# Activation parts and every work buffer behind them start 128 bytes higher in on-chip memory; no instruction is added, removed or reordered

## The reference, cut to what matters

```
h      = modulate(rms_norm(x)), modulate(rms_norm(ctx))      # modulation: silu(c) @ mod_w
x     += gate * rms_norm(gated_linear_attention(h))          # 4 heads, both directions, ctx state first
x     += gate * rms_norm(silu(h @ W_gate) * (h @ W_up) @ W_out)      # hidden width 2816
---- second block
proj   = (x * (1 + scale) + shift) @ w_in                    # 9232 columns
o_a    = gated_deltanet(conv(qkv_a), ...)                    # 8 heads, triangular solve per chunk
o_b    = chunk_band_attention(q_b, k_b, v_b, rel_bias)       # 16 heads
x      = layernorm(alpha * x + gate * ((g_a * o_a @ Wa + g_b * o_b @ Wb) @ w_o))
x      = layernorm(alpha * x + gate * ((silu(u_gate) * u_val) @ w_down)),  u = conv(h @ w_up)
```

## Time and profile before

| | us |
|---|---|
| median of 3 runs | 1036.68 (1034.71 to 1036.95) |
| the profiled execution, its own time | 1037.48 |
| its span, first to last instruction | 1035.7 |
| granted TensorE clock, mean over the span | 0.972 of full |

### The profile page before, as it was taken

The page is one execution under the profiler, slowest core; times in us unless marked ns, Lnnn a source line. Parts: engine busy times, 40 slices in busy tenths (PEclk is TensorE's granted clock), DMA queues, the critical chain, the costliest instruction groups (busy, mean ns, idle before and its releaser), DMA issues.

```text
span 1035.7 us, 19911 instructions
## 1 busy us (share of the span) xinstructions
PE 955.3 (92%) x8438; PEld 903.5 (87%) x8438; DVE 702.7 (68%) x1112; ACT 547.3 (53%) x829; POOL 27.0 (3%) x71
## 2 busy tenths in 40 slices
PE   4699999969999999799899999989998699999995
PEld 1489999869999999699699998978998499999994
DVE  2659937677777665888774543566568778888744
ACT  2658232654544435756736334466764466766434
POOL 2100000000000000400100000000000000000000
PEclk9899999989999999899999999999999799999997
DMA  9834656548888887257424336543457545656921
GB/s 333 283 102 148 246 197 211 196 131 272 278 271 277 286 274 265 82 182 250 130 91 145 124 129 147 184 144 122 140 188 248 177 130 178 196 185 199 326 91 41
DMA packets 57400, 196.78 MB, mean 190 GB/s; under 512 B 6096, under 2 KB 10592, under 8 KB 57056
## 3 DMA queue, kind: packets, MB, share of 16 engines
q1 hardware_dynamic: 51840, 187.72, 54.2%
q10 hardware_dynamic: 5216, 7.53, 2.8%
q0 software_dynamic: 256, 0.26, 0.1%
HBM read 194.43 MB, written 1.06 MB: 189 GB/s over the span
## 4 chain that ended last, share of the span: by engine, by line
PE 76%; DVE 13%; ACT 5%; DMA 2%; issue 2%; ACTq 0%; SPq 0%; DVEq 0%
PE panel_banks L399 65%; DVE w_lo L1460 3%; DVE mix_work L1802 3%; DMA raw<-in_panels 2%; PE work_banks L768 2%; ACT w_hi L946 2%; DVE raw L1493 1%; PE work_banks L596 1%; PE work_banks L697 1%; PE work_banks L739 1%; PE work_banks L556 1%; PE work_banks L529 1%; PE work_banks L851 1%; PE work_banks L796 1%; ACT gla_work L984 0%
## 5 line engine op out<-in xcount | busy, mean ns | idle before, releaser
L399 PE MATMUL panel_banks<-act_hi,w_hi 128*128 128x256 f32 (+1 forms) x1600 | 462.0, 289 | 25.9 <-DVE w_lo L1460 10.1
L399 PE MATMUL panel_banks<-act_lo,w_hi 128*128 128x256 f32 (+1 forms) x1600 | 454.0, 284 | 0.0
L399 PE MATMUL panel_banks<-act_hi,w_lo 128*128 128x256 f32 (+1 forms) x1600 | 453.5, 283 | 0.0
L1460 DVE TENSOR_TENSOR w_lo<-raw,w_hi 128x1024 fp32r<-128x1024 f32 x260 | 315.5, 1222 | 141.6 <-ACT w_hi L946 140.9
L946 ACT ACTIVATE w_hi<-raw 128x1024 fp32r<-128x1024 f32 x260 | 272.3, 1055 | 164.0 <-PE panel_banks L399 121.7
L399 PEld LDWEIGHTS panel_banks<-act_hi,w_hi 128*128 128x128 f32 x1600 | 303.8, 190 | 38.5 <-issue 20.7
L399 PEld LDWEIGHTS panel_banks<-act_lo,w_hi 128*128 128x128 f32 x1600 | 304.4, 190 | 1.9 <-issue 0.5
L399 PEld LDWEIGHTS panel_banks<-act_hi,w_lo 128*128 128x128 f32 x1600 | 303.9, 190 | 1.6
L399 PE MATMUL panel_banks<-hidden_hi,w_hi 128*128 128x256 f32 x352 | 98.6, 280 | 2.4 <-ACT hidden_hi L1165 2.4
L399 PE MATMUL panel_banks<-hidden_hi,w_lo 128*128 128x256 f32 x352 | 98.4, 279 | 0.0
L399 PE MATMUL panel_banks<-hidden_lo,w_hi 128*128 128x256 f32 x352 | 98.2, 279 | 0.0
(11 more groups left out here) (268 smaller groups left out, 974.7 us busy)
## 6 DMA issues: line engine op xcount, KB each, us to landing
raw<-in_panels SPq DMA_DIRECT2D x356, 512.0 KB, 5.1
mix_work<-delta_rows ACTq DMA_DIRECT2D x2, 1024.0 KB, 11.9
x_t<-in_x ACTq DMA_DIRECT2D x1, 1024.0 KB, 9.4
gla_work<-in_ctx_x ACTq DMA_DIRECT2D x1, 1024.0 KB, 14.5
mix_work<-in_rel_bias ACTq DMA_DIRECT2D x1, 1024.0 KB, 10.2
out_x<-ffn_work SPq DMA_DIRECT2D x4, 256.0 KB, 2.5
mix_work<-in_rel_bias ACTq DMA_DIRECT2D x1, 768.0 KB, 14.9
c_wide<-in_c_rows ACTq DMA_DIRECT2D x1, 512.0 KB, 4.0
```

The lines of the kernel that those rows point to most:

```text
L399: ins = pe.matmul(out_, a, b, start=start and p == 0, stop=stop and p == 2, skip_group_check=True)
L1460: dve.tensor_tensor(wlo[:, v_ % PARTS, :], raw[:, u % RAW, :], whi[:, v_ % PARTS, :].bitcast(F32), ALU.subtract)\
```

## The change

The unused tensor in front of the activation parts grows from 16 to 48 numbers:

```
-        sb("act_home", [P, 16])
+        sb("act_home", [P, 48])
```

## The result

| | before | changed |
|---|---|---|
| median, us | 1036.72 (1034.61 to 1038.37, 6 runs) | 1028.57 (1022.76 to 1031.02, 6 runs) |
| ratio | | 0.9911, 95% interval 0.9891 to 0.9931 |
| the profiled execution, its span | 1037.48, 1035.7 | 1027.39, 1025.6 |
| granted TensorE clock, mean | 0.972 | 0.966 |

The forecast was 1036.7 us, "no change that can be measured". The kernel became 0.9% faster. The time lies in the range, but the kernel did change, and clearly beyond the interval, where no change was forecast.

The account below looks back on a forecast made before the run. The kernel was taken to be bound by the number of matmuls times the distance between their starts. Terms (a), (b) and (c) were each 0, so 1037.5 us profiled, 1036.7 us as median, range 1024 to 1041.5 us.

Parts of the forecast that it names:

- term (a): Distance between three-pass matmul starts, one operand moved, weights not: change taken as 0, bounds +4.3 to -23.6 us.
- Nothing about the addresses changed there: In qkv near 490 us the rate slowed after one matmul some 15 ns late; so rate is a state.
- Two relations, 320 and 192, thus give the same pair of rates: Moved minus unmoved address modulo 512, in normal and swapped panels: both show fast and slow rates, supporting 0.
- Each instruction sweeps over all remainders wherever it starts: Moving tiles of 1,024 bytes and weight blocks of 512 cover all remainders modulo 512, supporting 0 for layout.
- (b): Duration of DVE and ACT instructions on moved buffers: taken as 0, bounds ±0.2 to ±2.2 us.
- (c): DMA transfers into moved buffers: taken as 0; DMA's whole share of the chain would be 21 us.
- Fast stretches are lost: Rival: restarts after other PE work leave the matmuls in the slow rhythm, +4.3 us, 1041.0 us; chance 0.12.
- One or two long stretches turn fast: Rival: long slow stretches such as ffn_in's 1,050 matmuls take the fast rhythm, 1028 to 1032 us; chance 0.10.
- The rhythm is a matter of layout after all: Rival: the new address relation is fast nearly everywhere, 1013 to 1024 us, about 1018; chance 0.11.
- A third, slower distance: Rival: weight and activation read streams disturb each other more, up to +27.9 us, 1064 us; chance 0.07.

Follow-up runs that it names:

- p256: Kernel before with the activation parts and all behind them 256 bytes higher; 1036.32 us, ratio 0.9993.
- p0: Kernel before without the unused tensor, activation parts and all behind them 64 bytes lower, operand distance 0 modulo 256; 1048.79 us, ratio 1.013.
- d112_act: Kernel before with act and hidden parts starting 48 bytes inside larger tensors, weights left at 128 modulo 256, distance 112; 1025.04 us, on repeat 1023.31 us.
- stream_map: Kernel without its computation, only bursts of 72 three-pass matmuls at 16 operand distances, other engines idle; 113.3 to 120.0 ns per matmul.
- work_only: Kernel before with only the work space (gla_work, hidden, ffn_work, mix_work) 128 bytes higher, act_hi and act_lo unmoved; 1035.96 us, ratio 0.9996.

## Why the prediction was wrong, point by point

**What bounds the kernel: right.** Matmul count times distance, with two rhythms 4.4 ns apart. All of the gain is there.

**The step that failed is term (a), "I take 0 for this term".** It rested on three arguments. "Nothing about the addresses changed there", so the rate is a state: true, and shown again by the changed kernel's three profiles. But the late matmul of the earlier trace rows was read as the cause of the slow rhythm, and the same one, later still, left the stream fast after the change. "Two relations, 320 and 192, thus give the same pair of rates": also true as read, and too little. Modulo 256, the period that p256 shows, the new relation of 448 is the 192 of the swapped panels, so the trace of before did hold it. There 345 of 576 matmuls were fast, at the other relation 640 of 5,760. That imbalance was the signal, and I counted which rates occur instead of how often. (The fast windows from 648.7 and 663.3 us in the earlier trace rows are swapped panels too; the prediction counts them as fast stretches only.) "Each instruction sweeps over all remainders wherever it starts": this was the real mistake. The starts count all the same, as p0 at 120.0 ns and d112_act at 113.3 show. One way to see it is that two streams that sweep at one pace keep their distance; no trace shows their pace. The term measured -13.3 us instead of 0, inside the bounds of -23.6 to +4.3 us that I had set, and 10.1 us of it reached the span.

**The rule on the read ports.** The row came first: two rates at one clock. The Trainium skill's page "TensorE: Matmul & The Clock Gate" ("What happens when you issue a matmul") has two independent read ports for weights and moving operand, and "SBUF — State Buffer" ("SBUF: two separate sides") has TensorE wait for no other engine. I kept the rule from excluding a layout effect, and still took the value that it gives. What I drew from the two ports, that placement costs nothing, doesn't hold: in stream_map the pair of load and matmul took 113.3 to 120.0 ns by the distance of its operands. Whether the ports wait for one another there, or something behind them, no run shows. The second half isn't contradicted: 113.3 ns is reached in stream_map with the other engines idle and in `ffn_in` with DVE, ACT and DMA busy.

**Terms (b) and (c): right.** DVE and ACT stayed within 0.1% in their busy time; DMA isn't needed for the rhythms, since stream_map shows the rates with it all but idle.

**The rivals.** "Fast stretches are lost" happened only in the swapped panels and was outweighed. "One or two long stretches turn fast" had the size, 1028 to 1032 us. "The rhythm is a matter of layout after all" had the mechanism, at 0.11, but not the size: the new distance makes the fast rhythm available, and the three profiles of the changed kernel still have 2,061, 2,725 and 2,793 distances in the slow one, the swapped panels' among them. "A third, slower distance" was given 0.07 with "nothing speaks for it"; it exists at other shifts, 118.7 and 120.0 ns.

**The share given back.** I had priced stretches by 4.4 ns per matmul without a loss. About a quarter was given back, mostly at half the clock. That this follows from the faster matmuls isn't shown: work_only, slow in four windows of five, had a mean clock of 0.963, lower than the changed kernel's 0.966. So -13.3 us is what the rhythms were worth in this pair of profiles, and -8.2 us is what the medians show.

What stays open is what picks the rhythm after a restart, and why the pattern has a period of 256 bytes and a grain of 16 to 32. No run here looks inside the pipe.

## What to carry to other kernels

When matmuls run back to back and each brings its own weights, compare the distance between starts with the best that occurs in the same trace at the same clock; two rates for one instruction are a finding, not noise. Count how often each occurs, by the relation of the operands' addresses. Then sweep the placement of one operand in steps of 32 bytes (and 16, inside a larger tensor) with an unused tensor in front: it costs up to a few hundred bytes per partition and was worth from +1.3% to -1.2% here. Judge a placement by several profiles and stretches, since a burst by itself, or one profile, can show a rhythm that the next execution doesn't take.

## What the runs showed of the hardware that was not expected

- A weight load of 128 x 128 with a 256-column float32r matmul repeats every 113.3 ns at best, and every 116.7 to 120.0 ns at other distances of the two operands (stream_map), at a granted clock of 1.00 and with every other engine idle.
- Two rhythms can be stable at one place, 113.3 and 117.8 ns: the same program came out with `ffn_in` in the one in its first profile and in the other in the next two. One matmul that came late in both kernels was followed by the slow rhythm at distance 64 and by the fast one at 192.
- At distance 112 with the weights at 128 modulo 256, all ten windows of two profiles ran at 113.3 ns; with the weights at 80 modulo 256, the same distance gave 120.0 ns in four windows and 116.7 in one.
- Moving both operands together by 128 bytes changes nothing that can be measured (0.9992, interval 0.998 to 1.0004), and moving one by 256 neither (0.9993, interval 0.9979 to 1.0008).
